# Seven block products instead of eight in the z chunks of a hybrid attention layer

## The reference, cut to what matters

```python
h = rmsnorm(x, g_norm)
proj = jnp.einsum('bsd,de->bse', h, w_in)
(m_q, m_k, m_v, m_z, n_q, ..., n_g, n_z) = jnp.split(proj, _split_points(), axis=-1)
...
y_moba = rmsnorm(o_moba * jax.nn.silu(m_z), g_out_moba)
y_nsa = rmsnorm(o_nsa * jax.nn.silu(n_z), g_out_nsa)
y = jnp.concatenate([y_moba, y_nsa], axis=-1)
return x + jnp.einsum('bse,ed->bsd', y, w_out)
```

## Time and profile before

| | |
|---|---|
| median of 3 runs | 500.39 us (500.28 to 500.43) |
| the profiled execution | 500.16 us |
| its span, first to last instruction | 498.4 us |
| busy, share of the span: PE / DVE / ACT / POOL | 98% / 62% / 48% / 12% |
| DMA | 96.44 MB, 194 GB/s |

### The profile page before, as it was taken

One profiled execution on the slowest core, in us unless ns is written; L12 is line 12 of the kernel. 1 busy time (PEld: TensorE's weight loads), 2 busy tenths in 40 slices (PEclk: granted clock), 3 DMA queues, 4 the chain that ended last, 5 costly groups with the idle time before them and its releaser, 6 DMA issues.

```text
span 498.4 us, 6394 instructions
## 1 busy us (share of the span) xinstructions
PE 489.3 (98%) x2524; PEld 407.2 (82%) x2524; DVE 309.9 (62%) x503; ACT 239.5 (48%) x339; POOL 57.6 (12%) x66
## 2 busy tenths in 40 slices
PE   8999999999999999999999999999999999999993
PEld 7888778787788888888888888888888888888883
DVE  5886644345789949756676845645666565745452
ACT  5784335353556444554453445536436553445421
POOL 2340101001111202000020200003212030022020
PEclk9999999999999999999999999999999999999998
DMA  8989779685353442443344244445964456366212
GB/s 292 332 276 379 270 273 326 203 286 183 126 207 107 169 168 86 168 170 118 136 168 161 95 168 170 170 164 202 366 212 153 173 198 221 109 229 237 101 68 101
DMA packets 54478, 96.44 MB, mean 194 GB/s; under 512 B 4304, under 2 KB 13104, under 8 KB 54064
## 3 DMA queue, kind: packets, MB, share of 16 engines
q1 hardware_dynamic: 54416, 96.03, 55.5%
q10 hardware_dynamic: 32, 0.01, 0.0%
HBM read 93.93 MB, written 2.10 MB: 193 GB/s over the span
## 4 chain that ended last, share of the span: by engine, by line
PE 96%; issue 2%; DVE 0%; POOL 0%; ACT 0%; POOLq 0%; ACTq 0%; DVEq 0%
PE proj L524 26%; PE proj L526 26%; PE proj L525 26%; PE b_o L782 4%; PE b_t L505 2%; PE b_p L751 2%; PE b_s L651 2%; PE proj L558 2%; PE proj L564 1%; PE proj L569 1%; PE b_s L526 1%; PE b_s L524 1%; PE b_s L525 1%; PE proj L806 1%; PE b_s L711 0%
## 5 line engine op out<-in xcount | busy, mean ns | idle before, releaser
L1112 DVE TENSOR_TENSOR w_lo<-w_raw,w_hi 128x2048 fp32r<-128x2048 f32 x72 | 166.6, 2315 | 102.4 <-ACT w_hi L855 102.3
L524 PE MATMUL proj<-w_hi,xT_hi 128*128 128x512 f32 x504 | 198.6, 394 | 0.0
L526 PE MATMUL proj<-w_hi,xT_lo 128*128 128x512 f32 x504 | 196.5, 390 | 0.0
L525 PE MATMUL proj<-w_lo,xT_hi 128*128 128x512 f32 x504 | 196.3, 390 | 0.0
L855 ACT ACTIVATE w_hi<-w_raw 128x2048 fp32r<-128x2048 f32 x72 | 137.7, 1913 | 45.4 <-PE proj L526 34.0
L524 PEld LDWEIGHTS proj<-w_hi,xT_hi 128*128 128x128 f32 x504 | 94.7, 188 | 20.5 <-issue 1.6
L526 PEld LDWEIGHTS proj<-w_hi,xT_lo 128*128 128x128 f32 x504 | 94.6, 188 | 20.2
L525 PEld LDWEIGHTS proj<-w_lo,xT_hi 128*128 128x128 f32 x504 | 94.7, 188 | 18.6
L958 ACT ACTIVATE pT<-b_p 128x512 f32<-128x512 f32 (+2 forms) x24 | 11.8, 492 | 61.9 <-PE b_p L751 61.9
L472 POOL TENSOR_TENSOR rope_a<-rope_a,rope_b 128x512 f32<-128x512 f32 (+1 forms) x12 | 13.1, 1110 | 160.2 <-DVE rope_b L1199 160.2
L524 PE MATMUL proj<-w_hi,ymT_hi 128*128 128x512 f32 x64 | 25.0, 390 | 0.0
(11 more groups left out here) (226 smaller groups left out, 492.8 us busy)
## 6 DMA issues: line engine op xcount, KB each, us to landing
w_raw<-in_w_in_dram SPq DMA_DIRECT2D x57, 1024.0 KB, 4.9
w_raw<-in_w_out_dram SPq DMA_DIRECT2D x16, 1024.0 KB, 5.0
xo<-in_w_ck_dram SPq DMA_DIRECT2D x4, 1024.0 KB, 7.8
xo<-in_w_cv_dram SPq DMA_DIRECT2D x4, 1024.0 KB, 7.8
w_raw<-in_w_in_dram SPq DMA_DIRECT2D x12, 256.0 KB, 6.7
Q<-in_x_dram SPq DMA_DIRECT2D x1, 2048.0 KB, 9.5
out_dram<-Q SPq DMA_DIRECT2D x8, 256.0 KB, 2.8
xo<-in_x_dram SPq DMA_DIRECT2D x3, 512.0 KB, 7.8
```

Source lines behind the costliest of these rows:

```text
L524: nc.tensor.matmul(dst, a_hi, b_hi, start=first, stop=False)
L525: nc.tensor.matmul(dst, a_hi, b_lo, start=False, stop=False)
L526: return nc.tensor.matmul(dst, a_lo, b_hi, start=False, stop=last)
L1112: nc.vector.tensor_tensor(wl, w_raw[:, u % RAW], wh.bitcast(F32), ALU.subtract).then_inc(lo_ready, 1)
```

## The change

The first four k tiles of two z chunks a, b (pair 0 is chunks 11 and 12, pair 1 is 13 and 14) are seen as a 2 x 2 block product: tokens in two halves, k in two halves (two k tiles each), columns in two chunks. Before, it is eight block products (the units (a, 0) and (b, 0), 48 products). After, it is a seven product scheme (P1 to P7), each block product 2 k tiles x 3 = 6 products, 42 in all. It needs four sums of x blocks, made once (`x_sums`, slot 38; rounded and its residue in slot 40), and for each pair four sums of weight blocks (`t1` to `t4`) on DVE. The four weight blocks (0.5 MB each) have loads and buffers of their own. Seven weight operands, numbered n = 0 to 6, are split by ACT (`block_hi`) and DVE (`block_lo`) in three items of the ring of split buffers: early (n = 0, 1), middle (2, 3) and late (4, 5, and 6 in the place of 4).

There are 72 units now: unit numbers count the plain ones. Units 0 to 43 are as before; 44 to 46 are chunk 11's (its g = 1, 2, 3), 47 to 49 chunk 12's, 50 to 52 chunk 13's, 53 to 55 chunk 14's, and 56 to 71 the output projection.

PE's order with s0 = 44 (pair 0) and 52 (pair 1):
- slot s0 - 2, early: P1 (n = 0), P5 (n = 1); for pair 0 then unit 42. Slot 50 has no unit.
- slot s0 - 1: unit 43 or 49.
- slot s0, middle: P6 (n = 2) and P3 (n = 3), which add to the banks of P1 and P5 after ACT has copied those (`mid_out_`, copies 0 and 1), then chunk a's g = 1 unit (44 or 50) for the first token half.
- slot s0 + 1, late: P7 (n = 4), after ACT's copy 2 of the bank with P6 in it; P2 (n = 5); after copy 3, which waits for P7, the second token half of unit 44 or 50; P4 (n = 6, whose split waits for P7).
- then units 45 to 48 in slots 46 to 49; 51 to 54 in 54 to 57; slot 58 is empty; 55 in slot 59; unit s - 4 from slot 60.

The banks end without a part of the sum that ACT copied out (scaled by rstd). So silu is now: DVE adds rstd * bank and the copy, ACT takes the sigmoid of that from SBUF (`sigmoids`), DVE multiplies; POOL waits for `z_ok`. The squares' unused output goes to another tile, since `raw_e`, `nv` and `vpad` now hold weight blocks.

```diff
+PAIRS = [(11, 12, 44), (13, 14, 52)]
+SEVEN = {"P1": ("x", 0, 0, 1, 0, True), "P5": ("s", 2, 1, 0, 1, True), "P6": ("s", 0, 0, 1, 2, False), "P3": ("s", 2, 0, 0, 3, False),
+         "P7": ("s", 0, 1, 1, 4, False), "P2": ("x", 2, 0, 2, 5, True), "P4": ("x", 2, 1, 3, 6, True)}
...
+ROUNDED_AT = {41: 42, 42: 43, 43: 44, 44: 45, 45: 46, 46: 47, 47: 48, 49: 49, 50: 50, 52: 51, 53: 52, 54: 53, 55: 54, 56: 55, 57: 56, 58: 57}
...
 SP
+                if u == 42:
+                    block(0, 0)
+                if u == 43:
+                    sp.wait_ge(pv_done, NH)
+                    block(0, 1)
+                    block(0, 3)
+                if u == 44:
+                    sp.wait_ge(xs_lo_ok, 1)
+                    block(0, 2)
+                if u == 50:
+                    sp.wait_ge(blk_lo, 7)
+                    for n in range(4):
+                        block(1, n)
...
-                if u == 54:
+                if u == 56:
                     sp.wait_ge(scores_done, len(JOBS))
+                    sp.wait_ge(mid_done, 6)
                     sp.dma_start(acc, x[0].rearrange("(m p) c -> p m c", p=P)).then_inc(acc_in, 16)
-                if u == 56:
-                    sp.wait_ge(pv_done, 2 * NH)
+                if u == 60:
+                    sp.wait_ge(dve_read, dve_reads(NC - 1))
...
 PE
+            def seven(p, name):
+                of, k0, m, bank_no, n, new = SEVEN[name]
+                pe.wait_ge(blk_lo, 7 * p + n + 1)
...
+            def pair_late(p):
+                a, b, _ = PAIRS[p]
+                pe.wait_ge(mid_out, 4 * p + 3)
+                seven(p, "P7").then_inc(mid_done, 1)
+                bank_free(b)
+                seven(p, "P2")
+                pe.wait_ge(mid_out, 4 * p + 4)
+                unit_rows(UNIT_NO[a, 1], 1).then_inc(unit_used, 1)
+                seven(p, "P4").then_inc(unit_used, 1)
...
 ACT
+            def sigmoids(i):
+                n = CHUNKS[i][2]
+                act.wait_ge(pt_done, len(JOBS))
+                if n:
+                    act.wait_ge(z_ok, 2 * n)
+                for m in range(MT):
+                    act.wait_ge(dve_read, dve_reads(i - 1) + m + 1)
+                    nc.scalar.activation(sig[:, m, :], (rope_a, rope_b)[n % 2][:, m, :], ACT.Sigmoid).then_inc(sig_ok, 1)
...
+                if slot == 40:
+                    xs_round()
+                for p in range(len(PAIRS)):
+                    s0 = PAIRS[p][2]
+                    if slot == s0 - 4:
+                        block_hi(p, 0)
+                        block_hi(p, 1)
+                    if slot == s0 - 2 and p:
+                        block_hi(p, 2)
+                        block_hi(p, 3)
+                        mid_out_(p, 0)
+                        mid_out_(p, 1)
+                    if slot == s0:
+                        block_hi(p, 4)
+                        mid_out_(p, 2)
+                        block_hi(p, 5)
+                    if slot == s0 + 1:
+                        mid_out_(p, 3)
+                        block_hi(p, 6)
+                if slot and rounded_at(slot) is not None and rounded_at(slot) < NU:
+                    hi(rounded_at(slot))
+                if slot == PAIRS[0][2] - 2:
+                    mid_out_(0, 0)
+                    mid_out_(0, 1)
+                    block_hi(0, 2)
+                    block_hi(0, 3)
...
+                if slot % UPC == UPC - 1 and slot < NPROJ and KINDS[slot // UPC] == "z":
+                    sigmoids(slot // UPC)
...
 DVE, silu
                 for m in range(MT):
-                    dve.wait_ge(act_read, act_reads(i - 1) + m + 1)
-                    nc.vector.scalar_tensor_tensor(z[:, m, :], proj_b[i % 2][m][:, :], rstd[:, m:m + 1], z[:, m, :],
-                                                   ALU.mult, ALU.mult).then_inc(dve_read, 1)
+                    nc.vector.scalar_tensor_tensor(z[:, m, :], proj_b[i % 2][m][:, :], rstd[:, m:m + 1], copies[m],
+                                                   ALU.mult, ALU.add).then_inc(dve_read, 1)
+                for m in range(MT):
+                    dve.wait_ge(sig_ok, 2 * n + m + 1)
+                    nc.vector.tensor_tensor(z[:, m, :], z[:, m, :], sig[:, m, :], ALU.mult).then_inc(z_ok, 1)
...
 DVE, the loop
+                if slot == 38:
+                    x_sums()
+                if slot == 40:
+                    xs_residual()
+                for p in range(len(PAIRS)):
+                    s0 = PAIRS[p][2]
+                    if slot == s0 - 4:
+                        block_lo(p, 0)
+                        t1(p)
+                        block_lo(p, 1)
+                    if slot == s0 - 2 and p:
+                        block_lo(p, 2)
+                        block_lo(p, 3)
+                    if slot == s0:
+                        block_lo(p, 4)
+                        block_lo(p, 5)
+                    if slot == s0 + 1:
+                        block_lo(p, 6)
+                if slot > 1 and rounded_at(slot) is not None and rounded_at(slot) < NU:
+                    lo(rounded_at(slot))
+                if slot == PAIRS[0][2] - 2:
+                    block_lo(0, 2)
+                    block_lo(0, 3)
+                for p in range(len(PAIRS)):
+                    if slot == PAIRS[p][2] - 3:
+                        t2(p)
+                    if slot == PAIRS[p][2] - 1:
+                        t3(p)
+                        t4(p)
```

More of the change, by code:

```diff
@@ L53, with stream, plain, used @@
 OUT_DONE = [NPROJ + max(i for i, u in enumerate(OUT_UNITS) if u[0] == c) for c in range(3)]
+PAIRS = [(11, 12, 44), (13, 14, 52)]
+PAIR_OF = {c: p for p, pair in enumerate(PAIRS) for c in pair[:2]}
+SEVEN = {"P1": ("x", 0, 0, 1, 0, True), "P5": ("s", 2, 1, 0, 1, True), "P6": ("s", 0, 0, 1, 2, False), "P3": ("s", 2, 0, 0, 3, False),
+         "P7": ("s", 0, 1, 1, 4, False), "P2": ("x", 2, 0, 2, 5, True), "P4": ("x", 2, 1, 3, 6, True)}
+SUMS_SLOT = 38
+def stream():
+    units, ring = [], []
+    def plain(c, g):
+        ring.append(("unit", len(units)))
+        units.append((c, g))
+    first = PAIRS[0][0]
+    for u in range(first * UPC - 2):
+        plain(u // UPC, u % UPC)
+    ring.append(("early", 0))
+    plain(first - 1, 2)
+    plain(first - 1, 3)
+    for p, (a, b, _) in enumerate(PAIRS):
+        ring.append(("middle", p))
+        plain(a, 1)
+        ring.append(("late", p))
+        plain(a, 2)
+        plain(a, 3)
+        plain(b, 1)
+        plain(b, 2)
+        if p + 1 < len(PAIRS):
+            ring.append(("early", p + 1))
+        plain(b, 3)
+    for c, g in OUT_UNITS:
+        plain(NC + c, g)
+    return units, ring
+UNITS, RING = stream()
+NU = len(UNITS)
+RING_NO = {r: n for n, r in enumerate(RING)}
+UNIT_NO = {u: n for n, u in enumerate(UNITS)}
+def used(u):
+    return RING_NO["unit", u] + 1
+def used_by_chunk(c):
+    return used(UNIT_NO[c, UPC - 1])
+def unit_at(slot):
+    for p, (a, b, s0) in enumerate(PAIRS):
+        if s0 <= slot < s0 + 2 * UPC:
+            return {2: UNIT_NO[a, 2], 3: UNIT_NO[a, 3], 4: UNIT_NO[b, 1], 5: UNIT_NO[b, 2], 7: UNIT_NO[b, 3]}.get(slot - s0)
+    return slot if slot < PAIRS[0][2] else slot - (NSLOT - NU)
+ROUNDED_AT = {41: 42, 42: 43, 43: 44, 44: 45, 45: 46, 46: 47, 47: 48, 49: 49, 50: 50, 52: 51, 53: 52, 54: 53, 55: 54, 56: 55, 57: 56, 58: 57}
+def rounded_at(slot):
+    if slot < 40:
+        return slot + 2
+    return ROUNDED_AT.get(slot) if slot < 60 else slot - 2
 OUT_SLOT = OUT_DONE[:2] + [OUT_DONE[2] + 2]
@@ L814, in _ @@
             for slot in range(LAST):
-                unit(slot)
+                for p in range(len(PAIRS)):
+                    if slot == PAIRS[p][2] - 2:
+                        pair_early(p)
+                    if slot == PAIRS[p][2]:
+                        pair_middle(p)
+                    if slot == PAIRS[p][2] + 1:
+                        pair_late(p)
+                if unit_at(slot) is not None:
+                    unit(unit_at(slot))
                 if slot == 2:
@@ new lines, in block_hi @@
+            def block_hi(p, n):
+                if n in (0, 3, 5):
+                    act.wait_ge(blk_in[{0: 0, 3: 2, 5: 3}[n]], 16 * (p + 1))
+                else:
+                    act.wait_ge(blk_sum, 4 * p + {1: 1, 2: 2, 4: 3, 6: 4}[n])
+                if n == 6:
+                    act.wait_ge(mid_done, 3 * p + 3)
+                else:
+                    act.wait_ge(unit_used, RING_NO[("early", "middle", "late")[n // 2], p] - SPL + 1)
+                nc.scalar.activation(block_split(p, n)[0], block_raw(n), ACT.Copy).then_inc(blk_hi, 1)
```

181 lines of the change are left out of this document (137 added, 44 removed).

## The result

The kernel after takes **505.19 us** (504.14 to 505.40, five runs), the kernel before 500.29 us beside it. The ratio is 1.0091, 95% interval 1.0077 to 1.0106: slower, by more than the 0.2% that a measurement tells from no change. The profiled execution took 504.46 us, where that of before took 500.16.

The account below looks back on a forecast made before the run. PE was taken as bound only by the number and spacing of its products: twelve fewer give -2.72 us, pair 1's delay +5.7, together +3.0, so 503.4 us for the median, range 500.2 to 506.8.

Parts of the forecast that it names:

- which wait, where, and from what: Pair 1, slot 53: P7 waits for DVE's residue 4, behind silu of chunk 12; PE stands 3.8 to 4.9 us.
- pair 0 gives its 1.36: Slots 44 and 45: P7 and P4 fed with slack 0.5 to 1.0 us, no stall, so 1.36 us saved.
- the prices: Half-unit splits and residues of 1,024 columns, by straight line between rows: 1.06 us on ACT, 1.22 on DVE.
- full exclusion: POOL and two-input DVE instructions shut each other out whole; pair 1's delay is then 6.1 us, without any 5.4.
- the late end: Residue 4 ready at 18.5 us after zero if POOL's multiply holds it, against 17.4 without.
- the second wait: Unit 50's second half waits for ACT's last copy, starting at 21.7 or 22.4, 5.4 to 6.1 us late; 5.7 taken.
- the clock: Rival: the stand before P7 halves the granted clock, 1.2 to 4 us more, 504.5 to 507.5 us; chance 0.25.
- the forecast proper: Pair 1's delay of 5.7 us without a clock fall: 503.4 us median; chance 0.47.
- the forecast's own case: Pair 1's delay without a clock fall, with slope error on ten chained operations: 502.2 to 504.8 us.
- the full gain: Rival: slot 52's splits reach DVE in time, so all 2.72 us is saved: 497.7 us (497 to 499); chance 0.15.

Follow-up runs that it names:

- e1: The kernel after, with pair 1's third and fourth weight sums moved ahead of unit 50's residue on DVE: 502.98 us, ratio 1.0053.
- e3: The kernel after, with chunk 12's sigmoids behind splits 4, 5 and unit 51's on ACT, and DVE's multiplies behind residue 5: 508.49 us, ratio 1.0163.
- e4: The kernel after with seven products for pair 0 only, chunks 13 and 14 multiplied as before: 499.34 us, ratio 0.9981.
- e2: The kernel after, with 16 unread identity products on PE during the wait before pair 1's P7: 504.02 us, ratio 1.0072.
- e6: e3 with the last copy in a buffer of its own, ahead of the two squares: 504.55 us, ratio 1.0079.
- e5: The kernel after, with pair 1's sums, multiplies and sigmoids reordered on DVE and ACT and the last copy in its own buffer: 500.27 us, ratio 1.0000.
- e8: e5 with POOL's products of chunk 12 held until unit 51's residue, and y's first transposes a slot back: 500.43 us, ratio 1.0005.
- e9: e5 with unit 51's residue and residue 6 ahead of DVE's multiplies, and y's first transposes a slot back: 499.97 us, ratio 0.9993.
- e7: e1 with 8 unread identity products on PE before pair 1's P7: 502.18 us, ratio 1.0037.

## Why the prediction was right, and where it was off

**Right: which wait, where, and from what.** P7 of pair 1 on DVE's residue of block 4, behind silu of chunk 12. Zero, the start of the product behind slot 49's unit, is 349.70 in the kernel after. The third and fourth sums were to end at 12.2 and 13.4 and ended at 12.1 and 13.2 (361.78, 362.91); silu's first step at 14.7, and it ended at 14.5; P7 was to start at 17.4 to 18.5 and started at 18.3, the end with POOL's share. e1 and e3 show that it is this chain: shorten it by two sums and P7 comes 1.6 earlier; move silu's sigmoids and multiplies out of it and it comes 2.4 earlier.

**Right: pair 0 gives its 1.36.** No wait there, and e4 shows the gain alone, less 0.16 at the start.

**Right: the prices.** 1,024 columns were estimated at 1.06 on ACT and 1.22 on DVE, and took 1.04 to 1.06 and 1.22.

**Right: POOL and DVE.** By full exclusion P7 was to be at the late end, and was. The Trainium skill ("SBUF — State Buffer", section "SBUF: two separate sides") says that a DVE instruction with two SBUF inputs and a GpSimd one shut each other out for a whole instruction. The traces agree: 1.98 or 3.36 for a residue beside POOL's products, 1.23 and 2.28 with those held back.

**Off: the second wait.** The step "it starts at 21.7, or 22.4 with POOL's share (residue 5 late for P2)", 5.4 to 6.1 us after the half's due time; the 21.7 was the last copy's. The copy ended at 371.25, 21.6 after zero, to the tenth as worked out. But that half's due time had moved: P7's delay, then P2's own wait for residue 5 (0.6 in e2), had brought it to 371.7 without any clock (372.18 in e2, where PE was 0.48 late). The copy was never the last to come. The half began at 372.45, 6.15 late, and the sum had 5.7 for it. That 5.7 is so near is in part luck: without the clock the half would have begun 5.4 late (371.7 for 366.30), by P7's and P2's waits for residues 4 and 5 and not by the copy, and the clock added 0.75.

**Off: the clock.** It had a chance of 0.25 and a price of 1.2 to 4, and it came; the forecast proper, without it, had 0.47. The measured 505.19 lies above the 502.2 to 504.8 of the forecast's own case and in the 504.5 to 507.5 of the clock's, which the whole range took in. The step that failed is the argument against it, that a stand of 3.8 is hardly over the 3.3 us of rest after the last product. The fall after the end of the work is one event, and it says nothing of a shorter rest: in e1 a stand of 2.0 us was enough. Its price, 1.2 to 4 us, was too high for this execution, 0.75 net by e2: it was down for most of twelve products, not for 24, and P2's wait lay beneath the slow ones. The Trainium skill ("TensorE: Matmul & The Clock Gate", section "HAM oscillation — how this bites in real kernels") warns of such waits between bursts; this trace now shows it in the midst of a kernel, 0.61 and 0.54.

**Left out: half a microsecond at the end.** No step had the last store, and it is 0.5 of the 1.8 us by which the median was under the measured 505.19. The rest are 0.45 in the delay (6.15 for 5.7), 0.4 in small waits, and 0.5 in the step from the profiled execution to the median (505.19 - 504.46 = 0.73, where I added 0.23).

**A slip.** Under the full gain, 8.2 + 4.3 is 12.5 and not 12.7. It changes neither the rival nor its chance.

## What to carry to other kernels

Work that is "hidden" on a half idle engine is hidden only if its place in that engine's queue is: write out, with times, the queue of each engine around the first use of each new operand, and look for an instruction in it that waits for something late. When one such wait is cured, its followers move with it, and the next bound is found in the same list; here the order that gets 2.0 us out of seven products instead of eight came after seven that do not (the kernel after, e1, e3, e6, e5, e8, e9). Take out first what a cured step now collides with (here POOL's products against DVE's residues).

## What the runs showed of the hardware

- **The clock.** PE stood for 4.3 us (the kernel after), for 2.0 us (e1) and for 2.4 us (e6), and in all three the granted clock fell only after work had begun again, by 0.4, 0.9 and 0.7 us, and was whole again by 372, 371 and 378. In e3's long wait (5.3 us) it fell during the stand. After stands of 1.6 (e5), 1.8 (e8) and 1.3 us (e9) it stayed at 1.00 throughout the profiled executions. One other execution of e8 took 502.53 us at a mean granted clock of 0.991, where the other ten took at most 500.75 at 0.994 to 0.996; it has no timeline, so whether the clock fell behind the stand there is not shown. Small matmuls of the identity in the stand kept the clock at 1.00 and gave 1.2 us (e2) and 0.8 us (e7) in the medians.
- **DVE and POOL.** Beside POOL's products a residue of 2,048 columns took 3.16 us (the kernel before) to 3.38 for 2.28, one of 1,024 columns 1.98 to 2.32 for 1.22; POOL's pair of products took 3.88 to 4.95 beside such residues (the kernel after, e3, e5, e6) and 2.55 alone (e8).
- **Open: the last store.** In every kernel with two pairs it lands 0.5 us later after its issue than in the kernel before and in e4. The one other thing that goes with it in the pages is the instruction queue q14, 11 packets in the former and 10 in the latter. Whether one causes the other was not tried.
